# Attention: TensorE multiplies the probabilities of one unit with V ahead of, not behind, the transposes of the next unit

## The reference, cut to what matters

```python
s = jnp.einsum('brnihd,brnmhd->brnhim', qb, kw) * (Dh ** -0.5)
s = s - slopes[:, None, None] * dist
s = jnp.where(valid[:, None], s, NEG_INF)
lse = jax.nn.logsumexp(s, axis=-1)
p = jnp.exp(s - lse[..., None])
o = jnp.einsum('brnhim,brnmhd->brnihd', p, vw)
...
alpha = jax.nn.softmax(jnp.stack(lses, axis=0), axis=0)
o = jnp.concatenate([outs[g] * alpha[g][..., None] for g in range(N_GROUPS_A)], axis=2)
```

## Time and profile before

| | |
|---|---|
| median of 3 runs | 2043.32 us (2042.5 to 2045.5) |
| the profiled execution | 2045.53 us, of which its span is 2043.7 us |
| TensorE busy | 2008.1 us, 98% of the span |
| VectorE, ScalarE, GpSimd busy | 1245.5 us (61%), 943.2 us (46%), 337.0 us (16%) |
| mean granted TensorE clock | 0.996 |

### The profile page before, as it was taken

How to read it: one execution, slowest core, us unless ns; L and a number is a source line. 1 busy time by engine, 2 the same in 40 slices (tenths; PEclk the granted TensorE clock), 3 DMA queues, 4 the chain that set the end, 5 groups by cost and what they waited for, 6 DMA issues and landing times.

```text
span 2043.7 us, 24674 instructions
## 1 busy us (share of the span) xinstructions
PE 2008.1 (98%) x9316; PEld 1657.5 (81%) x9316; DVE 1245.5 (61%) x1687; ACT 943.2 (46%) x1445; POOL 337.0 (16%) x238
## 2 busy tenths in 40 slices
PE   8999899998999999999999999999999999999999
PEld 8988567887888888888888888788788888888887
DVE  5288785588776777634536344549877776753433
ACT  6233687645555554423434532334555555542231
POOL 0022100352223223000102000125223223200000
PEclk9999999999999999999999999999999999999999
DMA  5111000412532232444443211141252332244444
GB/s 173 31 42 31 28 17 9 146 52 71 167 93 75 81 93 73 144 142 152 139 165 107 79 41 32 52 144 51 73 175 68 87 93 74 78 160 145 148 140 175
DMA packets 193646, 196.50 MB, mean 96 GB/s; under 512 B 32768, under 2 KB 147968, under 8 KB 193536
## 3 DMA queue, kind: packets, MB, share of 16 engines
q1 hardware_dynamic: 193392, 194.81, 30.7%
q10 hardware_dynamic: 144, 0.21, 0.0%
HBM read 159.33 MB, written 35.65 MB: 95 GB/s over the span
## 4 chain that ended last, share of the span: by engine, by line
PE 82%; issue 12%; DVE 3%; ACT 2%; POOL 0%; POOLq 0%; ACTq 0%; DVEq 0%
PE bank L790 21%; PE bank L791 21%; PE bank L792 21%; PE bank L546 4%; PE bank L547 4%; PE bank L548 4%; PE bank L648 1%; PE bank L649 1%; PE bank L650 1%; PE bank L731 1%; PE bank L712 1%; DVE bl L1451 1%; PE bank L699 1%; PE bank L928 1%; ACT pT L1095 0%
## 5 line engine op out<-in xcount | busy, mean ns | idle before, releaser
L790 PE MATMUL bank<-bh,spl 128*128 128x512 f32 x1064 | 416.2, 391 | 10.7 <-ACT rstd L1200 5.7
L792 PE MATMUL bank<-bh,spl 128*128 128x512 f32 x1064 | 415.2, 390 | 0.0
L791 PE MATMUL bank<-bl,spl 128*128 128x512 f32 x1064 | 415.0, 390 | 0.0
L790 PE MATMUL bank<-hid_h,down_h 128*128 128x512 f32 x704 | 273.9, 389 | 0.0
L791 PE MATMUL bank<-hid_l,down_h 128*128 128x512 f32 x704 | 273.9, 389 | 0.0
L792 PE MATMUL bank<-hid_h,down_l 128*128 128x512 f32 x704 | 273.9, 389 | 0.0
L1451 DVE TENSOR_TENSOR hid_l<-hid_w,hid_h 128x1024 fp32r<-128x1024 f32 x88 | 107.8, 1225 | 269.6 <-ACT hid_h L1334 269.6
L790 PEld LDWEIGHTS bank<-bh,spl 128*128 128x128 f32 x1064 | 200.6, 188 | 55.2 <-ACT rstd L1200 6.6
L792 PEld LDWEIGHTS bank<-bh,spl 128*128 128x128 f32 x1064 | 200.4, 188 | 42.0
L791 PEld LDWEIGHTS bank<-bl,spl 128*128 128x128 f32 x1064 | 200.6, 189 | 41.2
L1334 ACT ACTIVATE hid_h<-hid_w 128x1024 fp32r<-128x1024 f32 x88 | 93.2, 1060 | 297.9 <-DMA down_w<-w_down 297.9
(11 more groups left out here) (217 smaller groups left out, 3767.5 us busy)
## 6 DMA issues: line engine op xcount, KB each, us to landing
raw<-w_up SPq DMA_DIRECT2D x88, 512.0 KB, 5.4
hid_w<-hidden_kept SPq DMA_DIRECT2D x88, 512.0 KB, 3.4
hidden_kept<-hidden SPq DMA_DIRECT2D x88, 256.0 KB, 2.3
down_w<-w_down SPq DMA_DIRECT2D x88, 256.0 KB, 3.8
x_kept<-x SPq DMA_DIRECT2D x16, 512.0 KB, 6.5
x<-x_kept SPq DMA_DIRECT2D x16, 512.0 KB, 8.7
gws<-w_in SPq DMA_DIRECT2D x32, 256.0 KB, 3.2
qws<-w_qkv SPq DMA_DIRECT2D x24, 256.0 KB, 3.8
```

Of the source, the lines that this page charges most:

```text
L790: mm(out, wh, ah, start=first, stop=False, skip_group_check=True)
L791: mm(out, wh, al, start=False, stop=False, skip_group_check=True)
L792: return mm(out, wl, ah, start=False, stop=last, skip_group_check=True)
```

## The change

In each step of TensorE's loop the call of `values`(n-3) stands ahead of `turn`(n-2); in step 3 it stands ahead of the `qk_norm` too. No other engine's program changes.

```diff
                 if n == 2:
                     qk_norm(0, QK_TILES * NS - 2)
+                if n >= 3:
+                    values(n - 3)
                 if 0 <= n - 2 < NUNIT:
                     turn(n - 2)
                 if n == 3:
                     qk_norm(0, QK_TILES * NS - 1)
-                if n >= 3:
-                    values(n - 3)
                 if n == NUNIT:
```

## The result

Over 20 runs each on one chip the changed kernel takes 2048.32 us in the median (2047.16 to 2049.46), the kernel before 2043.15 us (2042.3 to 2045.52). The medians lie 5.2 us apart; the ratio is 1.0024 with a 95% interval of 1.0017 to 1.003, which is 4.9 us slower, where 3.3 us were forecast. Four of the 20 runs of the kernel before lie at 2045.5 us, the others between 2042.3 and 2043.7, and the profiled execution whose rows stand above is one of the four.

The account below looks back on a forecast made before the run. TensorE, busy 34.53 of 35 us, was taken to bound the attention core, with ScalarE next. Steady waits +1.2, weight splits +0.2, start +0.4 and end +1.5 make +3.3 us on 2043.3: 2046.6 us, range 2043.0 to 2050.0.

Parts of the forecast that it names:

- The steady part: Attention core's repeating steps: ordinary ones cost nothing, those with an act1h pair add waits, +1.2 us.
- the end: Last steps: values(29) wait 1.49 us and values(31) 0.97 us for their copies, together +1.5 us.
- The cover of 0.09 us: Ordinary steps: one unit's scores cover the pT copy, ready 1.78 us after the turn's start, values 1.87 us after.
- The first rival: Ordinary steps: copy reaches values 0.2 us later than taken, so they wait too; 2050.0 us, chance 0.17.
- The fourth steps: Steps with an act1h pair between pT copies: values wait 0.43 us (even) or 0.49 us (odd), +1.2 us.
- The owh splits: Steps 8 and 9, where ScalarE also splits two weight tiles: a first wait of 0.19 us, +0.2 us.
- the start: Steps 3 to 8: last qk product 0.4 us sooner, turn(5) queued behind values(4) costs 0.8 us; +0.4 us.
- The rival of the clock: Last steps: new waits bring a low clock costing 1.7 us more, 2048.3 us, chance 0.13.
- The rival of the start's full gain: Start: turn(2) up to 1.7 us sooner, values(4) at full clock, about -2.5 us; 2043.7 us, chance 0.12.
- The signs: Expected in the new profile: turn(2) near 242 us (wrong if before 241), scores(8) 0.5 to 1 us later than 257.24.

Follow-up runs that it names:

- before_again: The kernel before, unchanged, profiled a second time in an execution of 2042.59 us; its runs took 2042.97 us, ratio 1.0001.
- after_again: The changed kernel, unchanged, for a second profile: 2049.11 us against 2043.16 for the kernel before, ratio 1.0027.
- the filled pair: Unused matmuls placed in TensorE's waits: kernel before with four in step 3, 2040.17 us; changed kernel with two more in step 7, 2043.94 us.
- old_tail: The changed kernel with its last three steps in the old order: 2051.27 us, ratio 1.0036 to the kernel before.
- the kernel with the copies apart in both its forms: Changed kernel with ScalarE's second act1h copy one step later, 2055.01 us; the same with VectorE's remainder also one step later, 2050.5 us.
- before: First profile of the unchanged kernel before, the one the forecast was summed from; that execution took 2045.53 us.
- old_step7: The changed kernel with step 7 in the old order, turn(5) ahead of values(4): 2047.36 us, ratio 1.002 to the kernel before.
- step3_pair_apart: Kernel before with values(0) moved ahead in step 3 and the two act1h copies in different steps: 2044.03 us, ratio 1.0001.
- steady_only: Kernel before with values ahead of turn only in steps 8 to 31: 2046.53 us, ratio 1.0016.
- step3_only: Kernel before with the new order in step 3 alone, values(0) ahead of the wait for GpSimd: 2041.09 us, ratio 0.9991.
- after_pair_apart: Changed kernel with ScalarE's second act1h copy of a group one step later, behind normed: 2055.01 us, ratio 1.0065 to the kernel before.

## Why the prediction was right and where it was wrong

The direction is right, and 2048.32 us lie within the outer range of 2043.0 to 2050.0. But they lie 0.7 us above the forecast's own band of 2045.6 to 2047.6, and the outer range reached up to 2050.0 for the failing cover, which did not happen. That the time falls inside is luck in this part. The steady part and the end were forecast for the right reasons, +2.6 us of the 4.65 by which the cores of the usual executions differ. The chances had a slip: with 0.17, 0.13, 0.12 and 0.03 for the others, the forecast had 0.55 left, not 0.58. The ratio of 1.0024 lies on the side of "slower by over 0.2%", to which I gave 0.34, though its interval reaches below 1.002.

**The cover of 0.09 us holds.** Ordinary steps have values 1.05 or 1.06 us behind scores in every profile of the new order with the act1h copies together. The first rival is out. The latency of 0.05 us that I took from a turn that waits for `normed` holds for values and their copy.

**The fourth steps** are right: 0.49 and 0.43 us forecast for odd and even, 0.50 and 0.43 found (1.03 and 0.96 less 0.53), and +1.21 us over scores(12) to scores(31) for the +1.2.

**The end** is right in its two waits, 1.49 and 0.97 us forecast and found; the whole end gives +1.37 us for +1.5. That it was passed on in full is shown by the 1705.4 to 1705.6 us behind it in both kernels.

**The owh splits** are a small miss with a wrong sign. The first wait is there (0.74 less 0.53 is 0.21 us for 0.19), but I took the old order as paying nothing new in steps 8 to 11, and it did pay. In `before_again` two turns wait 0.56 and 0.30 us between S8 and S12, and scores(9) 0.39; in `after_again` two values wait 0.21 and 0.29. From S8 to S12 the change gains 0.75 us in the filled pair (0.55 in the other, where scores(8) still run at low clock) for the 0.2 that I booked as lost.

**The failed step is the start, "+0.4 us", with its bounds of -1.5 and +0.8.** From scores(3) to scores(8) it measures +2.62 us (28.95 against 26.33). With the clock kept up it is +0.51 (25.27 against 24.76), which is the sum that I made: the product comes 0.29 us sooner for my 0.4, and the turn behind the wait costs 0.80. What I left out is the clock, and it enters at two places:

- Behind the wait of values(4). That wait was 1.88 us, it is 4.35 now, and in every profile that has one of over 4 us on the load row here (the change twice, `old_tail`, and the kernel with the copies apart in both its forms) the clock goes from 2.4 to 1.2 GHz between 253 and 255 us. In `after_again` values(4) and turn(5) take 1.74 and 1.47 us (254.44 to 256.18 to 257.65) instead of 1.02 and 0.80, 1.39 us more, and scores(8) behind them 1.24 us instead of 1.06, 0.2 more. Of the kernels with turn(5) inside the wait, some show a fall there (`before`, `old_step7`, `step3_pair_apart`) and some none (`before_again`, `steady_only`, `step3_only`). The Trainium skill (TensorE: Matmul & The Clock Gate, section "HAM oscillation") warns of matmul bursts with waits between them, behind which the array runs at half clock. The traces agree for this place.
- In step 4. Turn(2) comes 12.61 us after scores(3) in `after_again`, 11.89 in `before_again`, since the 6.8 us at low clock begin later there and reach into scores(4) and values(1): 0.72 us. That is the placement of one execution, not of the order: 11.95 us in the first profile after, 12.57 in the first before. It went the other way in the pair that I summed from.

Together that is the 2.31 us by which the two pairs differ at scores(12): +2.07 with the clock as it falls, -0.24 with it kept up. Each of the four numbers is one execution, and the low clock behind values(4) lasted 3.4 us in both profiles of the change but 10.2 in `old_tail`, which is the same kernel up to there; the size can differ by more than the 1.6 us that it has here.

**The rival of the clock** had the right mechanism and about the right price (+1.7 us), at a wrong place; that its "2048.3" is the measured median is luck. I put it in the last steps, where after a wait of 1.5 us the clock stayed at 1.00 in both profiles, and overlooked the wait that the change itself made long: the sum of the earlier trace rows already said that turn(5) leaves it. **The rival of the start's full gain** has its early turn(2) in the new order only when the clock is kept up: then it comes 10.3 us after scores(3), in both filled kernels, though S3 to S12 gains 0.24 us, not the 2.5 us that I priced: values(4) wait for VectorE all the same.

**The signs.** Some were named as times in the span, and the span's own start moves. Turn(2) came at 240.48 us in the first profile of the change, which by the text would be a sign of being wrong ("before 241 us"); but scores(3) came 0.83 us earlier too, and from scores(3) on it is 11.95 us against 12.57, so the turn stayed near its place as forecast. Scores(8) at 256.93 us, not behind 257.24, is the same effect: counted from scores(3) they are 0.52 us later.

**The base.** The sum was taken to the median through 2043.3, which was right. But the terms of the start were read from an execution of the 2045.5 us kind, in which values(4) already took 1.90 us at half clock. Between the two first profiles, which both have low clock behind values(4), the core grew by 2.62 us, between the usual ones by 4.65. Against the profile that I summed from, +0.52 us for the start looked right; against a usual execution the start's term is the one that fails.

## What to carry to other kernels

When an instruction that filled a wait is moved behind it, count it twice: once as work now queued behind the wait, and once for TensorE's clock in what follows, which must be priced at the wait that the change makes long, not where the profile was slow before. Read the placement of low clock in a second execution before a term is read from such a stretch. And a pipeline order could not be undone at one end alone here: where the order switches back, two dependent stages meet with nothing between them (2.31 us of wait here).

## What the runs showed of the hardware

- Low clock in the core lies at different places in different executions of one kernel (from 234.8 and from 231.7 us in the kernel before), and the core differs by 1.3 us with it.
- Matmuls whose result nobody uses can be worth their time where TensorE waits anyway: with six of them the changed kernel takes 2043.94 us instead of 2048.32 and 2049.11. With four the median of the kernel before falls by 2.6 us, but there the interval of the ratio (0.9982 to 1.0) reaches 1. The granted clock of the windows from 228 us on is 1.00 with them; without, it was 0.78 in the earlier trace rows and 0.86 and 0.90 in the windows after.
- Waits of 1.5 and 1.0 us among otherwise dense matmuls (328 to 342 us) did not lower the clock, nor did one of 1.7 to 1.9 us once in four units (`after_pair_apart`, clock 1.00 from 260 to 350 us); at a turn that waited 2.31 us it fell, in both kernels that had it (`steady_only`, `old_tail`).
